# Where the scalar engine waits for stored keys and values, and where a 3.3 MB load stands in the sync queue

## What is computed

```
h = rms_norm(x);  q, k, v, a, g = split(h @ w_in)
attn, new_k, new_v = attend(rms_norm(q), rms_norm(k), v)
c = silu(layer_norm(causal_depthwise(a * sigmoid(g))))
x = x + concat(attn, c) @ w_out
h = rms_norm(x)
x = x + (silu(h @ w_gate) * (h @ w_up)) @ w_down
```

## Time and profile before

| what | value |
|---|---|
| median of 3 runs | 1333.93 us (1332.3 to 1334.58) |
| the profiled execution, its own time | 1337.68 us |
| its span, first to last instruction | 1335.9 us |
| PE, DVE, ACT, POOL busy in the span | 98%, 50%, 24%, 32% |
| granted TensorE clock, mean over the span | 0.989 of full speed |
| HBM read and written | 120.09 MB and 43.28 MB |

### The profile page before, as it was taken

One profiled execution on the slowest core, in us unless ns is written; L12 is line 12 of the kernel. 1 busy time (PEld: TensorE's weight loads), 2 busy tenths in 40 slices (PEclk: granted clock), 3 DMA queues, 4 the chain that ended last, 5 costly groups with the idle time before them and its releaser, 6 DMA issues.

```text
span 1335.9 us, 22621 instructions
## 1 busy us (share of the span) xinstructions
PE 1306.2 (98%) x9120; PEld 1250.1 (94%) x9120; DVE 661.5 (50%) x1258; ACT 316.0 (24%) x716; POOL 425.4 (32%) x280
## 2 busy tenths in 40 slices
PE   9999999999997999999999999999999999999998
PEld 9999888888875899999999999999999999999998
DVE  7598898989884647811414131322223141414134
ACT  7212555445453444411010100000010101010100
POOL 2132432323210044255523424334243252432220
PEclk9899899999997999999999999999999999999999
DMA  8114153534372110782114101411124011410103
GB/s 253 52 52 154 32 165 112 169 113 156 100 246 80 33 64 17 261 291 93 48 48 158 64 32 46 164 46 57 39 87 135 32 48 48 158 64 32 40 1 134
DMA packets 50981, 131.07 MB, mean 98 GB/s; under 512 B 14512, under 2 KB 26928, under 8 KB 50352
## 3 DMA queue, kind: packets, MB, share of 16 engines
q1 hardware_dynamic: 45088, 95.34, 21.4%
q10 hardware_dynamic: 5792, 34.24, 7.5%
HBM read 120.09 MB, written 43.28 MB: 122 GB/s over the span
## 4 chain that ended last, share of the span: by engine, by line
PE 92%; DVE 3%; DMA 2%; issue 1%; ACT 1%; SPq 0%; POOL 0%; DVEq 0%; ACTq 0%; POOLq 0%
PE ps L355 28%; PE ps L357 27%; PE ps L356 27%; PE ps L777 1%; PE ps L746 1%; PE ps L812 1%; PE ps L819 1%; PE ps L796 1%; DMA out_nk_p<-zst 1%; PE ps L756 1%; PE ps L742 1%; DVE rb L1322 1%; PE ps L724 1%; DMA xr<-in_xT 0%; DVE ml_c L1654 0%
## 5 line engine op out<-in xcount | busy, mean ns | idle before, releaser
L642 POOL TENSOR_TENSOR wf<-raw,small 128x1024 fp32r<-128x1024 f32 x60 | 113.9, 1898 | 433.0 <-PE ps L357 423.3
L1687 DVE TENSOR_TENSOR pr<-ps,sg 128x362 f32<-128x362 f32 (+1 forms) x66 | 35.3, 536 | 411.0 <-ACT sg L1267 411.0
L355 PE MATMUL ps<-mh_a,wf 128*128 128x362 f32 (+1 forms) x624 | 208.3, 334 | 5.8 <-issue 2.9
L357 PE MATMUL ps<-mh_a,wf 128*128 128x362 f32 (+1 forms) x624 | 205.6, 329 | 0.0
L356 PE MATMUL ps<-ml_a,wf 128*128 128x362 f32 (+1 forms) x624 | 205.5, 329 | 0.0
L356 PE MATMUL ps<-ml_c,wf 128*128 128x362 f32 (+1 forms) x624 | 204.5, 328 | 0.0
L357 PE MATMUL ps<-mh_c,wf 128*128 128x362 f32 (+1 forms) x624 | 204.4, 328 | 0.0
L355 PE MATMUL ps<-mh_c,wf 128*128 128x362 f32 (+1 forms) x624 | 203.9, 327 | 0.0
L1307 DVE SCALAR_TENSOR_TENSOR uc<-uc,small 128x1024 f32<-128x1024 f32 x240 | 192.8, 864 | 0.3
L1705 DVE TENSOR_TENSOR y<-ps,y 128x362 f32<-128x362 f32 (+1 forms) x264 | 139.3, 534 | 107.9 <-PE ps L357 107.9
L1267 ACT ACTIVATE sg<-ps 128x362 f32<-128x362 f32 (+1 forms) x66 | 31.3, 474 | 620.5 <-PE ps L357 620.5
(11 more groups left out here) (162 smaller groups left out, 2076.5 us busy)
## 6 DMA issues: line engine op xcount, KB each, us to landing
raw<-in_w_stream SPq DMA_DIRECT2D x92, 512.0 KB, 3.6
skt<-in_kT_c SPq DMA_DIRECT2D x32, 384.0 KB, 4.9
sv<-in_v_c SPq DMA_DIRECT2D x32, 384.0 KB, 5.6
xr<-in_xT SPq DMA_DIRECT2D x8, 544.0 KB, 4.4
out_yT<-y SPq DMA_DIRECT2D x8, 544.0 KB, 2.7
y<-in_xT SPq DMA_DIRECT2D x1, 3264.0 KB, 16.4
out_nv_p<-vn SPq DMA_DIRECT2D x32, 64.0 KB, 1.7
out_nk_p<-zst SPq DMA_DIRECT2D x26, 64.0 KB, 1.6
```

Source lines behind the costliest of these rows:

```text
L355: e.matmul(out, wh, mh_, start=first, stop=False)
L357: return e.matmul(out, wl, mh_, start=False, stop=last)
L642: pool.tensor_tensor(hi(m), src, zeros, ALU.add).then_inc(w_hi, 1)
L1687: dve.tensor_tensor(pr[:, k6 % 2, 0:bn], bank(2 * (k6 % 2) + 1, bn), sg[:, k6 % 2, 0:bn], ALU.mult).then_inc(gu_pr, 1)
```

## The change

Two edits. On SP the 3,264 KB load into `y[2:8]` moves from ahead of the sample values' loads to behind the last keys' store. On ACT the waits for the stored values and keys move from ahead of `squares(0)` (s = 2) to ahead of `high(E0 + 3)` (s = 3), behind `squares(1)`. Nothing is added or removed. Line numbers from 484 to 1193 fall by one or two, since lines moved.

```
@@ sync
                 load_sk(2 * p + 1)
                 load_vfar(p)
-                if last:
-                    sp.dma_start(y[:, 2:KT, :], xT[2:KT].rearrange("k p n -> p k n")).then_inc(y_in[1], 16)
                 sp.wait_ge(d_pv, n0 + 1)
                 load_sv(2 * p + 1)
                 store(NT * p + NT - 1, "k")
                 if last:
+                    sp.dma_start(y[:, 2:KT, :], xT[2:KT].rearrange("k p n -> p k n")).then_inc(y_in[1], 16)
                     for n in range(E0 + 3, F0):
                         piece(n)
@@ scalar
                     if s == 2:
-                        act.wait_ge(v_st[NPAIR - 2], 16 * NT)
-                        act.wait_ge(k_st[0], K_ST[0])
-                        act.wait_ge(k_st[1], K_ST[1])
                         act.wait_ge(a_lo, 3)
                         squares(0)
                     if s == 3:
                         squares(1)
+                        act.wait_ge(v_st[NPAIR - 2], 16 * NT)
+                        act.wait_ge(k_st[0], K_ST[0])
+                        act.wait_ge(k_st[1], K_ST[1])
                         high(E0 + 3)
```

## The result

| | before | changed |
|---|---|---|
| median, first timing (4 runs each) | 1333.12 us | 1323.35 us (1321.69 to 1326.96) |
| ratio, 95% interval | | 0.993 (0.9906 to 0.9954) |
| median, timed once more (17 and 6 runs) | 1333.38 us | 1324.41 us (1321.33 to 1327.07) |
| ratio, 95% interval | | 0.9939 (0.9923 to 0.9954) |
| span of the profiled execution | 1335.9 us | 1325.2 us |

The change is faster by 0.6 to 0.7%, some 9 to 10 us; forecast were 11.0, with 1323.0 for the median.

The account below looks back on a forecast made before the run. PE was busy 98% of the span; its pause hung on the last keys' store, 14.19 us. Terms -8.08 - 3.21 + 0.32 = -10.97 us took the median from 1333.93 to 1323.0; range for 8 in 10: 1321.0 to 1327.0.

Parts of the forecast that it names:

- The first squares without the store: ACT's first squares no longer wait for the keys' store, so PE idles 0.70 instead of 8.78 ahead of "v" 0: -8.08 us.
- The clock: PE from "v" 0 to the turning of the probabilities runs at full clock, 3.85 instead of 7.06 us: -3.21 us.
- The added wait: ACT waits for piece 23 ahead of its high part, so PE's "v" 1 starts at 411.65 instead of 411.33: +0.32 us.
- The landing of piece 23: Weights in SP's queue: landing kept at 407.43, the same bytes ahead; up to 4.03 us later if the queue ran dry.
- The large load: Wanted by DVE's add of "e" 6 at 418.6, it lands before 407.4: 11 us of cover, no cost.
- The signs that named a time: Around the change: first squares before 396, "v" 0 about 404, "v" 1 under 412.
- With a pause of 0.70 I take the clock to stay at 1.00: PE's short pause ahead of "v" 0 leaves the clock full, since a pause of 1.49 us had; the 3.21 us rests on it.
- the rival of the fallen clock: PE's two short pauses, 0.70 and 0.32, still lower the clock, so 3.21 us are not won: 1326.2 us; chance 0.05.
- The Trainium skill's figure of about 358 GB/s: Bound on HBM to SBUF transfers per core; would put piece 23 some 2.2 us later and the time at 1325.2.

Follow-up runs that it names:

- kept_busy: The kernel before the change, its waits left in, with 50 unused matmuls filling PE's pause ahead of "v" 0; 1331.38 us, ratio 0.9984.
- copy_ahead: The changed kernel with one 2 MB cache copy taken from ACT's queue and issued by SP between the large load and piece 23; 1331.65 us, ratio 0.9992.
- pieces_first: The changed kernel with pieces 23 and 24 loaded ahead of the large load; 1322.16 us, ratio 0.992.
- full_again: The changed kernel, both edits, timed once more without alteration; 1324.41 us, ratio 0.9939.
- load_again: The kernel before with only the large load moved, timed a second time; 1324.59 us, ratio 0.9939.
- waits_only: The kernel before with only ACT's three waits moved, the large load left in its place; 1324.53 us, ratio 0.9935.
- load_only: The kernel before with only the large load moved, the three waits left ahead of the first squares; first timing 1327.78 us, ratio 0.9956.

## Why the prediction was right

- *The first squares without the store*: -8.08 forecast. Before, from the start of the values to "v" 0 it was 9.43 us (402.66 to 412.09), after 1.21 (404.40 to 405.61): -8.22.
- *The clock*: -3.21 forecast. After, "v" 0 to the turning took 3.83 us (405.61 to 409.44) instead of 7.06: -3.23. *kept_busy* shows the same term with the wait left in.
- *The added wait*: +0.32 forecast. From the turning to "v" 1 it took 3.97 us (409.44 to 413.41) instead of 3.47: +0.50. The mechanism is as forecast, the releaser too (the piece, not the store), and *copy_ahead* shows that it costs one for one from there.
- *The landing of piece 23*: taken as unmoved. It was: 14.97 us after its issue against 14.9. The queue did not stay as full as I argued. Read 1.66 us later than before, to take out the late start, the rate from 391.66 on was 206, 309 and 318 GB/s over three stretches of 2 us (DMA share 0.78, 0.90, 1.00), where it had been 236, 373 and 418 from 390 on (1.06, 1.00, 1.04). From 399.66 to 407.66 it was 407 to 414, where it had been 354 to 406 from 398 to 406. That these made up for the thin stretch fits the landing; it was not tried.
- *The large load*: 11 us of cover forecast. It landed at 407.9 (393.71 + 14.2), and no wait of DVE named it, in *pieces_first* neither, where it stands last.

The sum in the profile is -10.95 at "v" 1, forecast -10.97; that it is so close is in part luck, since the first term was 0.14 larger and the added wait 0.18 longer than forecast. The signs that named a time came as forecast once the 1.66 us are taken off by which this execution was late: the first squares at 394.95 (before 396 forecast), "v" 0 at 403.95 (404), "v" 1 at 411.75 (under 412).

The medians show less, 9.8 and 9.0 us. That the first of them, 1323.35, still lies 0.4 from the forecast 1323.0 is luck in part: the kernel before stood at 1333.12 in that timing, not at 1333.93. The step that was too sure is "With a pause of 0.70 I take the clock to stay at 1.00". Behind "v" 0 it did, in both profiled executions of the changed kernel. Behind "v" 1 it did in the first and not in the second (*full_again*):

```profile
407.47 0.80 PE L860 MATMUL ps<-ones_c,sq 128*128 128x1 f32 x6 [0.70 <-DVE sq L1442]
...
412.35 0.93 PE L767 MATMUL ps<-ident,tb 128*128 128x128 f32 x7
```
```profile
408.00:412.00 4.00, 4.00 (x30) 3.04 (x30) 2.36 (x6) 2.08 (x5) 0.85 (x1) 0.57 0.24 57
```

After a pause of 0.70 us the granted clock fell behind "v" 1, and from there to the next turning PE took 4.88 us (407.47 to 412.35) instead of 3.42. That is 1.46 us lost, of the size that the medians lack. *load_again* and *waits_only* show the same after 0.61 and 0.65; in *pieces_first*, without that pause, the clock stays. So the rival of the fallen clock, at a chance of 0.05, was right in part, but at another place and price than the 3.21 it named. How often this happens in the runs that were not profiled is not known. The medians of the granted clock rise from 0.992 in the 17 runs of before to 0.996 in the 6 of *full_again*, and within either kernel the runs of lower clock are by and large the slower ones (*full_again*: 1321.33 at 0.997, 1327.07 at 0.994).

One thing the prediction did not say: that either half would have done. It had both numbers for it (the store lands 8 us earlier by the load's move; piece 23 lands after the store in any case) and did not put them together. The Trainium skill's figure of about 358 GB/s ("DMA: Bandwidth & Descriptors", section "Where 436 GB/s comes from") is not borne out after either: 412 to 414 GB/s over 404 to 408.

## What to carry to other kernels

A wait belongs in front of the instruction that needs it, not in front of what happens to be issued earlier: here three waits held up squares that touch none of the memory they guard. When a small store lies on the chain, look at what was queued ahead of it; here either of two edits, moving the waiter or moving the load, did nearly all of it, and the next limit (the load of piece 23, last in the same queue) was the same for both. PE's pauses are worth more than their length if the clock falls in them: 8.2 us of pause carried 3.2 us of slow matmuls behind it, and 0.70 us carried 1.5 in *full_again*.

## What was not expected

A pause of the same length leaves the clock at full speed in one execution and halves it in another. Before, a pause of 1.49 us ahead of 395.78 left it at 1.00. In the first profile of *load_only* the same pause was followed by half clock:

```profile
397.27 0.44 PE L811 MATMUL ps<-pt,vn 128*64 128x128 f32 x4 [1.50 <-DVE ml_a L1459]
```
```profile
398.00:400.00 2.00, 2.00 (x8) 2.00 (x8) 1.82 (x9) 0.94 (x3) 0.00 (x0) 0.50 1.04 423
400.00:402.00 2.00, 2.00 (x25) 1.09 (x24) 0.82 (x3) 0.82 (x2) 0.00 (x0) 0.72 1.01 411
```

In *waits_only* half clock came behind "v" 1, as in *full_again*, after pauses of 0.54 us ahead of "v" 0 (which left it at 1.00) and 0.65 ahead of "v" 1:

```profile
407.87 0.82 PE L861 MATMUL ps<-ones_c,sq 128*128 128x1 f32 x6 [0.65 <-DVE sq L1443]
```
```profile
408.00:412.00 4.00, 4.00 (x32) 3.06 (x33) 2.53 (x7) 2.27 (x6) 0.85 (x1) 0.57 0.13 30
```

So one profile in which the clock held through a pause does not show that it holds. What decides it from run to run was not settled.
